# Hybrid decoder trunk on one core: output tile 10's weights loaded earlier, and the first down chunk in two passes

## The reference

```python
for l in range(2):
    h   = x @ w_in[l]                                  # 1024 -> 2560
    cat = heads(h)                                     # retention, HGRN2, sliding window; prompt and decode
    m   = cat @ w_out[l]                               # "output projection", 1024 -> 1024
    x   = layernorm(ALPHA * x + m, ln_mix)
    u   = relu(x @ w_up[l])                            # 1024 -> 4096
    x   = layernorm(ALPHA * x + (u * u) @ w_down[l], ln_ffn)   # 4096 -> 1024, "down"
```

## Time and profile before

| | |
|---|---|
| median of 3 runs | 2546.12 us (2541.11 to 2546.34) |
| the profiled execution's own time | 2550.04 us |
| its span, first to last instruction | 2548.1 us |
| mean granted clock of TensorE | 0.983 of full speed |
| TensorE, matmuls | 2429.4 us busy, 95% |
| VectorE / GpSimd / ScalarE | 64% / 43% / 39% |
| DMA over the span | 150 GB/s |

### The profile page before, as it was taken

The page is one execution under the profiler, slowest core; times in us unless marked ns, Lnnn a source line. Parts: engine busy times, 40 slices in busy tenths (PEclk is TensorE's granted clock), DMA queues, the critical chain, the costliest instruction groups (busy, mean ns, idle before and its releaser), DMA issues. The chain is left out here.

```text
span 2548.1 us, 45931 instructions
## 1 busy us (share of the span) xinstructions
PE 2429.4 (95%) x18822; PEld 2311.2 (91%) x18822; DVE 1629.9 (64%) x2556; ACT 983.4 (39%) x1779; POOL 1095.6 (43%) x1014
## 2 busy tenths in 40 slices
PE   8999988899999999999999999887999999999998
PEld 8998876688999999999999988766989999999997
DVE  3126778646855566878741367785488555677777
ACT  3226556433322223333432365564442222333333
POOL 0026767621455553344200277576315555534350
PEclk9999999889999999999999999998999999999999
DMA  5443222272233368567543523231722333865765
GB/s 183 155 150 111 94 75 79 68 201 89 76 111 102 101 229 292 177 250 270 195 154 135 166 92 96 73 95 53 219 80 77 103 110 114 290 241 190 283 230 173
DMA packets 290881, 381.08 MB, mean 150 GB/s; under 512 B 29296, under 2 KB 206768, under 8 KB 290640
## 3 DMA queue, kind: packets, MB, share of 16 engines
q1 hardware_dynamic: 290672, 378.14, 44.9%
HBM read 302.46 MB, written 77.66 MB: 149 GB/s over the span
## 5 line engine op out<-in xcount | busy, mean ns | idle before, releaser
L1356 PE MATMUL ps<-hid_hi,wd_hi 128*128 128x272 f32 (+1 forms) x1536 | 438.6, 286 | 6.8 <-DVE hid_lo L3174 6.8
L1358 PE MATMUL ps<-hid_hi,wd_lo 128*128 128x272 f32 (+1 forms) x1536 | 438.6, 286 | 0.0
L1357 PE MATMUL ps<-hid_lo,wd_hi 128*128 128x272 f32 (+1 forms) x1536 | 438.0, 285 | 0.0
L1356 PEld LDWEIGHTS ps<-hid_hi,wd_hi 128*128 128x128 f32 x1536 | 290.3, 189 | 7.4 <-issue 7.3
L1358 PEld LDWEIGHTS ps<-hid_hi,wd_lo 128*128 128x128 f32 x1536 | 290.5, 189 | 0.0
L1357 PEld LDWEIGHTS ps<-hid_lo,wd_hi 128*128 128x128 f32 x1536 | 289.8, 189 | 0.0
L3557 POOL TENSOR_TENSOR wd_lo<-wd_raw,wd_hi 128x2048 fp32r<-128x2048 f32 x38 | 181.1, 4767 | 239.7 <-ACT wd_hi L2376 239.7
L3551 POOL TENSOR_TENSOR wq_lo_S<-ws,wq_hi_S 128x512 fp32r<-128x512 f32 x104 | 194.2, 1876 | 115.8 <-ACT wq_hi_S L2439 115.8
L3529 POOL TENSOR_TENSOR wl_lo<-wl_raw,wl_hi 128x2048 fp32r<-128x2048 f32 x14 | 66.2, 4728 | 385.0 <-ACT wl_hi L2107 385.0
L1357 PE MATMUL ps<-wi_lo,u_hi 128*128 128x320 f32 x600 | 186.0, 310 | 0.0
L1358 PE MATMUL ps<-wi_hi,u_lo 128*128 128x320 f32 x600 | 185.3, 309 | 0.0
(11 more groups left out here) (373 smaller groups left out, 7487.9 us busy)
## 6 DMA issues: line engine op xcount, KB each, us to landing
wd_raw<-in_w_down SPq DMA_DIRECT2D x54, 1024.0 KB, 5.4
hid_raw<-hidscr SPq DMA_DIRECT2D x48, 1056.0 KB, 7.7
wq_raw<-in_w_up SPq DMA_DIRECT2D x26, 1024.0 KB, 5.9
wl_raw<-in_w_in SPq DMA_DIRECT2D x20, 1024.0 KB, 5.2
wi_raw<-in_w_in SPq DMA_DIRECT2D x15, 1280.0 KB, 6.7
hidscr<-h SPq DMA_DIRECT2D x32, 544.0 KB, 8.0
t_keep<-hidscr SPq DMA_DIRECT2D x16, 1056.0 KB, 12.3
hidscr<-h SPq DMA_DIRECT2D x32, 512.0 KB, 7.1
```

What stands on the lines that cost most here:

```text
L1356: nc.tensor.matmul(out, a_hi, b_hi, start=start, stop=False, skip_group_check=shared)
L1357: nc.tensor.matmul(out, a_hi, b_lo, start=False, stop=False, skip_group_check=shared)
L1358: return nc.tensor.matmul(out, a_lo, b_hi, start=False, stop=stop, skip_group_check=shared)
```

## The change

Two edits, in both layers.

1. **Tile 10 of the output projection.** SP issues `load_wo(l, 10)` in the decode step, behind the small cache stores and ahead of its wait for the decode states, and no longer in `attend_out`. The raw weights go into two pieces of their own, `wo_ahead`: one in the memory of `xn[0][1]` (the normalised tile of odd token tiles), one where `wo_raw1` (tiles 11, 13, 15) begins. ScalarE's and GpSimd's split of tile 10 is two instructions each, one per piece. Because of the shared memory, the load of tile 11 waits until tile 10 is split (before: tile 9), and VectorE's `center` of token tile 1 waits for that too.
2. **Chunk 0 of the down projection.** A new `down_start` waits first only for the high parts, runs the 32 high x high products of all four groups, then waits for the low parts and runs the other 64. In VectorE's `up`, both `q12` additions come ahead of both squares, and in the last block `hid_low(l, 1)` stands between them; it stood behind the squares.

```diff
+        wo_ahead = [place(f"wo_ahead{i}", [P, KT // 2, P], F32, at)[0] for i, at in enumerate((X0 + 129312, D0 + 32768))]
         def wo_raw(s):
-            return wo_in_lo[s % 2] if s < KT + 2 else wo_apart[s % 2]
+            if s == KT + 2:
+                return [(wo_ahead[i][:], slice(4 * i, 4 * i + 4)) for i in range(2)]
+            raw = wo_in_lo[s % 2] if s < KT + 2 else wo_apart[s % 2]
+            return [(raw[:], slice(0, KT))]
...
                 elif s >= KT + 2:
-                    sp.wait_ge(wo_hi_done, n - 1)
-                    sp.wait_ge(wo_lo_done, n - 1)
+                    done = n if s == KT + 3 else n - 1
+                    sp.wait_ge(wo_hi_done, done)
+                    sp.wait_ge(wo_lo_done, done)
...
+                load_wo(l, KT + 2)
                 sp.wait_ge(dd.sem, dd.at("h", l))
...
                 load_x(l, 0, 1)
-                load_wo(l, 10)
                 load_wo(l, 11)
                 load_x(l, 0, 2)
...
+            def down_start(l):
+                pe.wait_ge(wd_hi_done, wd_no(l, 0))
+                pe.wait_ge(hid_hi_done, hid_no(l, 0))
...
+                for g in range(4):
+                    for e in range(2):
+                        was = (("x40", "x40"), ("x41", "x41"), ("q210", "q211"), ("q120", "q121"))[g][e]
+                        pe.wait_ge(xd.sem, xd.at(was, seven_no(l, FBLOCKS - 1)))
+                        out, d, tok, side = place_of(g, e)
+                        for k in range(DCH):
+                            nc.tensor.matmul(out, wd_tile("hi", wd_buffer(0), k, d), hid_hi[0][:, k, tok],
+                                             start=k == 0 and (side == 1 or e == 0), stop=False, skip_group_check=side == 0)
+                pe.wait_ge(wd_lo_done, wd_no(l, 0))
+                pe.wait_ge(hid_lo_done, hid_no(l, 0))
+                for g in range(4):
+                    for e in range(2):
+                        out, d, tok, side = place_of(g, e)
+                        for k in range(DCH):
+                            nc.tensor.matmul(out, wd_tile("hi", wd_buffer(0), k, d), hid_lo[0][:, k, tok],
+                                             start=False, stop=False, skip_group_check=side == 0)
+                            last = nc.tensor.matmul(out, wd_tile("lo", wd_buffer(0), k, d), hid_hi[0][:, k, tok],
+                                                    start=False, stop=False, skip_group_check=side == 0)
+                    last.then_inc(down_ready, 1)
             def down(l):
-                for n in range(DSTEPS):
+                down_start(l)
+                for n in range(1, DSTEPS):
...
-                copy(wo_hi[q][:], wo_raw(s)[:]).then_inc(wo_hi_done, 1)
+                for raw, ks in wo_raw(s):
+                    last = copy(wo_hi[q][:, ks, :], raw)
+                last.then_inc(wo_hi_done, 1)
...
+                if t == 1 and not which:
+                    dve.wait_ge(wo_lo_done, 16 * l + KT + 3)
                 dve.wait_ge(na.sem, na.at("mean", n))
...
                     add("q12", s, "S4", quarter(s, 0, 1), u2[s][:])
+                if b + 1 == FBLOCKS:
+                    hid_low(l, 1)
+                for s in range(2):
                     dve.wait_ge(xd.sem, xd.at(f"q12{s}", n))
                     h = h_of[b % 2][s]
...
-                hid_low(l, 1)
                 for n in range(2, DSTEPS):
...
-                g_.tensor_tensor(wo_lo[s % 2][:], wo_raw(s)[:], wo_hi[s % 2][:], ALU.subtract).then_inc(wo_lo_done, 1)
+                for raw, ks in wo_raw(s):
+                    last = g_.tensor_tensor(wo_lo[s % 2][:, ks, :], raw, wo_hi[s % 2][:, ks, :], ALU.subtract)
+                last.then_inc(wo_lo_done, 1)
```

More of the change, by code:

```diff
@@ L629, in build @@
         xa = Steps(sem("seven_act"), "v0 v1")
-        xd = Steps(sem("seven_dve"), "x20 x21 q110 q111 x30 x31 q220 x40 q221 x41 q210 q211 q120 h0 q121 h1")
+        xd = Steps(sem("seven_dve"), "x20 x21 q110 q111 x30 x31 q220 x40 q221 x41 q210 q211 q120 q121 h0 h1")
         h_saved = [[sem(f"h_saved{q}{s}") for s in range(2)] for q in range(2)]
@@ L947, in load_wo @@
                 elif s >= KT + 2:
-                    sp.wait_ge(wo_hi_done, n - 1)
-                    sp.wait_ge(wo_lo_done, n - 1)
-                raw, S = wo_raw(s), wo_in[s % 2]
-                sp.dma_start(raw[:, 0:4, :], A["w_out"][l, 0:512, cols].rearrange("(k p) c -> p k c", p=P)).then_inc(S, 16)
+                    done = n if s == KT + 3 else n - 1
+                    sp.wait_ge(wo_hi_done, done)
+                    sp.wait_ge(wo_lo_done, done)
+                parts, S = wo_raw(s), wo_in[s % 2]
+                first, second = (parts[0][0][:, 0:4, :], parts[0][0][:, 4:8, :]) if len(parts) == 1 else (parts[0][0], parts[1][0])
+                sp.dma_start(first, A["w_out"][l, 0:512, cols].rearrange("(k p) c -> p k c", p=P)).then_inc(S, 16)
                 for kv in range(2):
-                    sp.dma_start(raw[64 * kv:64 * kv + 64, 4:8, :],
+                    sp.dma_start(second[64 * kv:64 * kv + 64, :, :],
                                  A["w_out"][l, 512 + 256 * kv:768 + 256 * kv, cols].rearrange("(g d) c -> d g c", d=64))\
@@ L1909, in down_group, with place_of @@
                 return done
+            def down_start(l):
+                pe.wait_ge(wd_hi_done, wd_no(l, 0))
+                pe.wait_ge(hid_hi_done, hid_no(l, 0))
+                def place_of(g, e):
+                    side, w = g // 2, SIDES[g // 2][1]
+                    at = (0, SIDES[0][1])[side]
+                    out = ps[:, 2 * g - 2 + e, 0:w] if side else ps[:, g, e * w:e * w + w]
+                    return out, 2 * (g % 2) + e, slice(at, at + w), side
+                for g in range(4):
[17 more added lines that the diff above has]
+                    last.then_inc(down_ready, 1)
             def down(l):
-                for n in range(DSTEPS):
+                down_start(l)
+                for n in range(1, DSTEPS):
                     i, c = divmod(n, DCHUNKS)
@@ L1923, in down @@
                         for e in range(2):
-                            if n == 0:
-                                was = (("x40", "x40"), ("x41", "x41"), ("q210", "q211"), ("q120", "q121"))[g][e]
-                                pe.wait_ge(xd.sem, xd.at(was, seven_no(l, FBLOCKS - 1)))
                             last = down_group(l, g, e, j,
@@ L3131, in up @@
                     add("q12", s, "S4", quarter(s, 0, 1), u2[s][:])
+                if b + 1 == FBLOCKS:
+                    hid_low(l, 1)
+                for s in range(2):
                     dve.wait_ge(xd.sem, xd.at(f"q12{s}", n))
                     h = h_of[b % 2][s]
-                    v.scalar_tensor_tensor(out=h[:], in0=h[:], scalar=0.0, in1=h[:], op0=ALU.max, op1=ALU.mult)                        .then_inc(xd.step(f"h{s}"), 1)
+                    v.scalar_tensor_tensor(out=h[:], in0=h[:], scalar=0.0, in1=h[:], op0=ALU.max, op1=ALU.mult)\
+                        .then_inc(xd.step(f"h{s}"), 1)
             def down_sums(l, n):
```

## The result

The changed kernel is slower: median 2559.7 us (2557.8 to 2563.5, four runs) against 2544.9 us (2541.1 to 2546.3, four runs), ratio 1.0055 with a 95% interval of 1.0042 to 1.0068, that is +14 us. The forecast was 2545.6 us, range 2537 to 2550.

A forecast was written before the change was run, and what follows sets the result against it. TensorE's matmuls, filling 95% of the span, were taken as the bound. Terms -3.4 + 0 + 0.95 + 0.75 + 1.2 = -0.5 us against the profiled 2550.0, which was 3.9 above the median, gave 2545.6 us; range 2537 to 2550.

The forecast's parts named there:

- Edit 1, the stall goes: Output projection, tile 10: waits of 4.24 and 1.92 us shrink, 0.2 to 0.4 us stay in the first layer, no clock fall.
- Tile 11's landing: Output projection: tile 11's load lands 3.0 to 4.0 us after its third DMA is issued, near 541.8 and 1807.3.
- Edit 1, what is late next: Output projection: tile 11's later load delays ScalarE's in-order queue, leaving a gain of 3.4 us in layer one, 0 in two.
- The third rival: Output projection: tile 11's reload takes 9 us to land, everything behind ScalarE's split 5.3 us later per layer; +10, chance 0.10.
- Edit 2: Down projection: chunk 1 starts 3.7 us earlier, but port turns delay the last store; chunk 4 starts 0.95 and 0.75 us later.
- The fall of the clock: Down projection: one fall of TensorE's clock in the two layers, costing 1.2 us, bounds 0 and 2.4.
- The `q12` order at nothing: Squares of the other 24 blocks move behind both `q12`: costs nothing, up to 0.1 us each if VectorE's pause is gone.

The follow-up runs named there:

- e1_raw_apart: Kernel before plus edit 1, with the raw buffer of tiles 11, 13 and 15 moved so tile 11's load doesn't wait for tile 10's split; ratio 1.0014.
- e1_wu_first: Kernel before plus edit 1, overlap left in, both y stores ahead of the wu loads, and `wu(0)` issued ahead of tile 11's load; ratio 1.0011.
- edit1_only: Kernel before with the tile 10 edit alone; ratio 1.0036, +9.2 us.
- e1_store_first: Kernel before plus edit 1, with y tile 0's store issued ahead of tile 11's load; ratio 1.0023, +5.9 us.
- stores_only: Kernel before with the stores of y tiles 0 and 1 ahead of `wu(0)` and `wu(1)`, neither edit; ratio 0.9998.
- e2_squares_first: Kernel before plus edit 2, with `hid_low(1)` back behind the squares; ratio 1.0013, +3.3 us.
- edit2_only: Kernel before with the chunk 0 and VectorE order edit alone; ratio 1.0019, +4.8 us.

## Why the prediction was wrong, step by step

- **Edit 1, the stall goes: right.** Foretold 0.2 to 0.4 us left, measured 0.17 and none. The gain was over-sized: the 4.24 us of the earlier trace rows was an unusually long draw. In the four other kernels that load tile 10 in the old place the stall is 1.5 to 3.2 us, and their first layer's stage is 60.6 to 61.9, not 63.18. Only one of their eight stalls brought a fall of the clock.
- **Tile 11's landing: right, or nearly.** Foretold 3.0 to 4.0 us after its third issue; it took 4.1 us in the first layer and 3.6 in the second. `root(2)` came at 1814.17, 2.6 us after that of the earlier trace rows, in a stage that had begun 3.0 later: all but unmoved, as foretold. In the first layer it came 1.1 us earlier in its stage, not 2.46: GpSimd ended tile 10's low part 0.6 us later in the stage than foretold, and the landing took 0.7 us more than the 3.4 in the sum.
- **Edit 1, what is late next: this step failed.** It followed tile 11's load into ScalarE's queue and stopped there. It did not follow it into SP's own queue, where x(2), `wu(0)`, tile 12 and the first y store stand behind the same wait. They went out in one burst, and tile 12 and the store arrived some 7 to 9 us after their issue. The sum had no wait at `again(2)`; it was 3.23 and 6.05 us, the second with a fall of the clock, for which the sum had no term either. -3.4 and 0 us were foretold; +0.65 and +7.4 were measured against the stages of before. Putting `wu(0)` ahead of that wait gave 6.6 us of stage time back in the two layers (with both stores moved), removing the wait 9.7.
- **The third rival** had the sign and nearly the size (+10), but in the wrong place: it made tile 11 itself slow and set tile 12 and `wu` aside because "they stand behind it". Standing behind was what made them late.
- **Edit 2: right in mechanism and near in size.** Turns at the port, last square at 16.2 us (foretold near 16), chunk 4's start 0.99 and 1.15 us later (foretold 0.95 and 0.75), new waits ahead of chunks 3 and 4. Chunk 1 gained 3.1 us, not 3.7. The fall of the clock was put on top of chunk 4's lateness with 1.2 us. There were two, of 1.7 us, but both lie between chunks 3 and 4 and made the wait for `hid_lo` ahead of chunk 4 shorter (0.48 us, not 2.5 to 2.9), so nothing came on top: the joints are +1.0 and +1.2, 2.2 against 2.9 foretold. Alone the edit had +4.5; there one fall came behind chunk 4's start and cost 1.6 us on top.
- **The `q12` order at nothing: right** (-0.8 us, interval -3.6 to +1.8).

Still open: e1_raw_apart and e1_wu_first have stages as long as those without edit 1, yet run 3.6 and 2.8 us above before, with intervals that begin at 0.3. No other stage of their profiles shows it, and a single profile can't, since executions of one kernel differ by up to 16 us. It is no constant price of edit 1: edit1_only and e1_store_first run 0.9 and 4.0 us below what their output projections say against 60.9.

## What to carry to other kernels

A wait put on one DMA is a wait for everything behind it on the issuing queue: list those transfers with their sizes, and ask for each whether it will now leave in the same burst as the others. Where something waits for a small store, it belongs ahead of a big load that nobody needs soon; where nothing does, moving it is worth nothing (stores_only, -0.5 us). When two engines take turns at a port, give way with the one whose result is needed last: a wait added to GpSimd turned a loss of 4.8 us into a gain of 6.6.

## What was unexpected of the hardware

- Waits of one length are followed by a fall of TensorE's clock in one stage and by none in another. The stretch from `back(4)` to the last up-product took 348.6 or 350.1 us (to 0.1) in all 26 stages of the thirteen profiles read, and nothing in between. All 26 have the same wait of TensorE, 2.15 to 2.18 us; in the fourteen longer ones the granted clock is 0.5 for 3.4 us behind it, in the twelve shorter ones it doesn't fall. In the profile of before the longer one is in the first layer, in that of after in the second. The fall in the first layer of before:

```profile
619.50:622.90 3.40, 3.40 (x19) 3.40 (x18) 1.23 (x1) 1.01 (x1) 0.00 (x0) 0.50 0.61 218
```

- At tile 10 too: a wait of 3.16 us brought no fall (e2_squares_first, first layer), one of 2.23 us did (edit2_only, first layer). So a sum like the prediction's can give such a fall only as a chance.
- The head steps vary by 5.4 us from one profile to the next: unit 8 of the first layer began between 517.1 and 522.5 us in the thirteen profiles read. The down stages with chunk 0 in one pass repeat within 0.5 us (15 of 16), the output projections without edit 1 within 1.4 (eight stages), so they tell what medians of a dozen runs could not.
